# A residual-stream norm: statistics token-major, scale and shift in fused multiplies, and the first two weight chunks interleaved by k tile

## The reference, cut to what matters

```python
def rms_norm(x, eps=EPS):
    xf = x.astype(jnp.float32)
    return (xf * lax.rsqrt(jnp.mean(xf * xf, axis=-1, keepdims=True) + eps)).astype(x.dtype)

def adaln(x, mod, k):
    return rms_norm(x) * (1 + mod[:, :, k + 1]) + mod[:, :, k]

def swiglu(h, w_in, w_out):
    g, u = jnp.split(h @ w_in, 2, axis=-1)
    return (jax.nn.silu(g) * u) @ w_out
# in each layer: ffn, mixer, ffn
h = h + 0.5 * mod[:, :, 2] * swiglu(adaln(h, mod, 0), ffn_in[i, 0], ffn_out[i, 0])
```

## Time and profile before

| | |
|---|---|
| median of 3 runs | 2378.21 us (2377.03 to 2379.68) |
| the profiled execution | 2379.09 us, span 2377.3 us, mean granted TensorE clock 0.942 |
| TensorE busy | 2146.5 us, 90% of the span (10458 matmuls) |
| VectorE, ScalarE, GpSimd busy | 1534.8, 718.7, 312.4 us |
| chain that ended last | TensorE 73%, VectorE 13%, issue 5%, DMA 3%, ScalarE 3%, GpSimd 2% |
| the three lines of `mm3` in that chain | 22% each |

### The profile page before, as it was taken

One profiled execution on the slowest core, in us unless ns is written; L12 is line 12 of the kernel. 1 busy time (PEld: TensorE's weight loads), 2 busy tenths in 40 slices (PEclk: granted clock), 3 DMA queues, 4 the chain that ended last, 5 costly groups with the idle time before them and its releaser, 6 DMA issues.

```text
span 2377.3 us, 26622 instructions
## 1 busy us (share of the span) xinstructions
PE 2146.5 (90%) x10458; PEld 1773.2 (75%) x10458; DVE 1534.8 (65%) x2030; ACT 718.7 (30%) x886; POOL 312.4 (13%) x243
## 2 busy tenths in 40 slices
PE   3979999997998887999998999999799787887998
PEld 2657888885877775888886788888587784477997
DVE  4767666678886557676577766677644548944544
ACT  1223322223220022322222323222354433433443
POOL 1221000112003232000012000011200004541001
PEclk7669999999999998999999999999899898989999
DMA  4453443553450023444354444354223312334554
GB/s 151 142 177 124 142 144 111 156 156 106 142 189 7 1 89 105 143 132 151 109 168 131 133 151 142 95 168 150 83 88 98 124 58 63 98 106 142 178 159 126
DMA packets 297501, 293.28 MB, mean 123 GB/s; under 512 B 8903, under 2 KB 260720, under 8 KB 296304
## 3 DMA queue, kind: packets, MB, share of 16 engines
q1 hardware_dynamic: 292928, 278.62, 37.3%
q10 hardware_dynamic: 4464, 13.15, 1.5%
HBM read 285.38 MB, written 6.36 MB: 123 GB/s over the span
## 4 chain that ended last, share of the span: by engine, by line
PE 73%; DVE 13%; issue 5%; DMA 3%; ACT 3%; POOL 2%; ACTq 1%; POOLq 0%; DVEq 0%; SPq 0%
PE bank L1509 22%; PE bank L1511 22%; PE bank L1510 22%; DVE pp L971 3%; DVE wl L893 2%; PE bank L1729 2%; ACT wh L578 2%; DMA raw<-in_ffn_out 2%; DVE pp L968 1%; DMA raw<-in_ada_w 1%; PE bank L1647 1%; DVE early_av L428 1%; POOL acc L1430 1%; PE bank L1797 1%; POOL mm L1492 1%
## 5 line engine op out<-in xcount | busy, mean ns | idle before, releaser
L1509 PE MATMUL bank<-xh,wh 128*128 128x512 f32 (+1 forms) x2120 | 785.7, 371 | 76.9 <-POOL xl L1413 37.8
L1510 PE MATMUL bank<-xl,wh 128*128 128x512 f32 (+1 forms) x2120 | 776.7, 366 | 0.0
L1511 PE MATMUL bank<-xh,wl 128*128 128x512 f32 (+1 forms) x2120 | 776.2, 366 | 0.0
L893 DVE TENSOR_TENSOR wl<-raw,wh 128x2048 fp32r<-128x2048 f32 (+1 forms) x204 | 421.4, 2067 | 303.1 <-ACT wh L578 302.8
L578 ACT ACTIVATE wh<-raw 128x2048 fp32r<-128x2048 f32 (+1 forms) x204 | 353.7, 1735 | 595.9 <-PE bank L1511 507.7
L1509 PEld LDWEIGHTS bank<-xh,wh 128*128 128x128 f32 x2120 | 408.0, 192 | 157.7 <-issue 39.5
L1511 PEld LDWEIGHTS bank<-xh,wl 128*128 128x128 f32 x2120 | 407.2, 192 | 63.9
L1510 PEld LDWEIGHTS bank<-xl,wh 128*128 128x128 f32 x2120 | 408.3, 193 | 61.4
L1509 PE MATMUL bank<-gh,wh 128*128 128x512 f32 (+1 forms) x704 | 255.6, 363 | 2.9 <-DVE wl L893 1.5
L1510 PE MATMUL bank<-gl,wh 128*128 128x512 f32 (+1 forms) x704 | 255.2, 362 | 0.0
L1511 PE MATMUL bank<-gh,wl 128*128 128x512 f32 (+1 forms) x704 | 255.2, 362 | 0.0
(11 more groups left out here) (219 smaller groups left out, 2213.4 us busy)
## 6 DMA issues: line engine op xcount, KB each, us to landing
raw<-in_ffn_in SPq DMA_DIRECT2D x88, 1024.0 KB, 5.1
raw<-in_ffn_out SPq DMA_DIRECT2D x64, 704.0 KB, 4.7
ada_rawf<-in_ada_w SPq DMA_DIRECT2D x60, 512.0 KB, 4.5
ada_rawo<-in_ada_w SPq DMA_DIRECT2D x48, 512.0 KB, 4.3
raw<-in_mb_in_w SPq DMA_DIRECT2D x24, 1024.0 KB, 5.4
raw<-in_ada_w SPq DMA_DIRECT2D x12, 1024.0 KB, 5.0
raw<-in_hy_in_w SPq DMA_DIRECT2D x12, 1024.0 KB, 5.1
afb<-decays SPq DMA_DIRECT2D x32, 256.0 KB, 3.2
```

What stands on the lines that cost most here:

```text
L893: dve.tensor_tensor(wl[n_slot][:, 0:cols], raw[r_slot][:, 0:cols], wh[n_slot][:, 0:cols].bitcast(F32), ALU.subtract).then_inc(w_lo, 1)
L1509: pe.matmul(dst, h, x_hi, start=start, stop=False)
L1510: pe.matmul(dst, h, x_lo, start=False, stop=False)
L1511: return pe.matmul(dst, l_, x_hi, start=False, stop=stop)
```

## The change

- The eighth square is no longer added by GpSimd. TensorE sums `acc` and the eighth square in two groups of matmuls, with the data as the stationary side and one column of ones as the moving one, so that a token's sum lies in its partition: 128x4 instead of 4x128. Square root and reciprocal work on 128x4; four transposes of a broadcast column fill `bank[7]`.
- VectorE makes `xt` = `hT` x scale x `bank[7]` in one fused operation for each half of the tokens (`scaled`), ScalarE makes `xh` as Identity with the shift as its bias, and VectorE, no longer GpSimd, makes `xl` = (`xt` + shift) - `xh` in place, fused as well (`low`). `xt` lies where `xl` lies, so there is no wait for slots of `pp`. VectorE's order is scaled(0), scaled(1), low(0), scaled(2), low(1) and so on.
- For "00", "hy", "01", "10", "mb" and "11" TensorE works off chunks 0 and 1 together (`first_pair`): for each k tile four output tiles, twelve matmuls. `SHARED = DT`: over all eight k tiles.
- Chunk 1 is split before the norm: its high half by ScalarE ahead of the square root, its low half by GpSimd (`second_lo`). In pair 0 of an FFN VectorE's first step is the low half of chunk 2. In `HYIN` and `XB` the halves of chunk 1 leave the first step of pair 0.
- The final norm's two operations a tile become one fused one.
- The loops of `XB`, of `wide` and of GpSimd's adds are unrolled.

```diff
@@ scalar
             def norm(key, n=NT):
...
-                act.activation(rs[0:j, 0:P], bank[7][0:j, 0:P], ACT.Sqrt, bias=eps[0:j, 0:1],
+                act.activation(rs[:, 0:j], bank[7][:, 0:j], ACT.Sqrt, bias=eps[:, 0:1],
                                scale=1.0 / D).then_inc(rms_done, 1)
-            def norm_hi(key, n=NT):
+            def norm_hi(key, layer, k0, n=NT):
                 pl = norms[key]
                 for k in range(DT):
-                    hi_tile(pl.q + k, pl.q + k + 1, xh[:, k, 0:n], pp[(pl.q + k) % 2][:, 0:n])
+                    act.wait_ge(p_ready, pl.q + k + 1)
+                    for w in range(n // L):
+                        ins = act.activation(xh[:, k, w * L:w * L + L], xt[:, k, w * L:w * L + L], ACT.Identity,
+                                             bias=mods[layer][:, DT * k0 + k, w:w + 1])
+                    ins.then_inc(p_hi, 1)
-            def ffn(key, ada, after, n=NT):
+            def ffn(key, layer, k0, ada, after, n=NT):
+                pi, po = ffn_in[key], ffn_out[key]
+                next_hi(pi, 0, 0, 2)
                 norm(key, n)
-                norm_hi(key, n)
+                norm_hi(key, layer, k0, n)
...
-                pi, po = ffn_in[key], ffn_out[key]
-                next_hi(pi, 0, 0, 2)
@@ vector
             def norm(key, layer, k0, n=NT):
...
+                def scaled(k):
+                    for w in range(n // L):
+                        tok = slice(w * L, w * L + L)
+                        ins = dve.scalar_tensor_tensor(xt[:, k, tok], hT[:, k, tok], m[:, DT * (k0 + 1) + k, w:w + 1],
+                                                       bank[7][:, tok], ALU.mult, ALU.mult)
+                    ins.then_inc(p_ready, 1)
+                def low(k):
+                    dve.wait_ge(p_hi, pl.q + k + 1)
+                    for w in range(n // L):
+                        tok = slice(w * L, w * L + L)
+                        ins = dve.scalar_tensor_tensor(xl[:, k, tok], xt[:, k, tok], m[:, DT * k0 + k, w:w + 1],
+                                                       xh[:, k, tok].bitcast(F32), ALU.add, ALU.subtract)
+                    ins.then_inc(p_lo, 1)
+                scaled(0)
                 for k in range(DT):
-                    q = pl.q + k
...
+                    if k + 1 < DT:
+                        scaled(k + 1)
+                    low(k)
...
                 def pair(i, last):
-                    next_lo(pi, i, 0, 2) if not last else split_lo((pi.w + 1) % 2, pi.w + FT, CW, (pi.raw + 1) % 2)
+                    if last:
+                        split_lo((pi.w + 1) % 2, pi.w + FT, CW, (pi.raw + 1) % 2)
+                    else:
+                        next_lo(pi, i, 0 if i else 1, 2)
...
-                    else:
+                    elif i:
                         next_lo(pi, i, 1, 2)
@@ gpsimd
-            def norm_lo(key, n=NT):
...
+            def second_lo(pl):
+                pool.wait_ge(raw_in[pl.raw % 2], (pl.raw // 2 + 2) * 16)
+                pool.wait_ge(w_hi, pl.w + 2)
+                n = (pl.w + 1) % 2
+                pool.tensor_tensor(wl[n][:], raw[(pl.raw + 1) % 2][:], wh[n][:].bitcast(F32), ALU.subtract).then_inc(w_lo, 1)
@@ tensor
             def norm(key, n=NT):
                 pl = norms[key]
-                pe.wait_ge(acc_done, pl.h)
...
+                cols = n // P
+                pe.wait_ge(acc_done, pl.h - 1)
+                for j in range(cols):
+                    pe.matmul(bank[7][:, j:j + 1], acc[:, j * P:j * P + P], ones[:, 0:1], start=j == 0, stop=False)
+                pe.wait_ge(sq_done, pl.h)
+                for j in range(cols):
+                    ins = pe.matmul(bank[7][:, j:j + 1], tt[1][:, j * P:j * P + P], ones[:, 0:1], start=False, stop=j == cols - 1)
...
                 pe.wait_ge(rms_inv, pl.norm + 1)
-                for j in range(rows_):
-                    ins = pe.matmul(bank[7][:, j * P:j * P + P], ident[0:rows_, j:j + 1].to_broadcast([rows_, P]),
-                                    rs[0:rows_, 0:P], start=True, stop=True)
+                for j in range(cols):
+                    ins = pe.transpose(bank[7][:, j * P:j * P + P], rs[:, j:j + 1].to_broadcast([P, P]), ident)
                 ins.then_inc(rms_bc, 1)
+            def first_pair(pl, q, n=NT):
+                def tiles(u, k):
+                    for s in range(2):
+                        ins = mm3(bank[2 * u + s][:, 0:n], (pl.w + u) % 2, k * 256 + s * P, xh[:, k, 0:n], xl[:, k, 0:n],
+                                  k == 0, k == DT - 1)
+                    if k == DT - 1:
+                        ins.then_inc(w_used, 1)
+                for k in range(DT):
+                    pe.wait_ge(p_lo, q + k + 1)
+                    for u in range(2 if k < SHARED else 1):
+                        if k == 0:
+                            pe.wait_ge(w_lo, pl.w + u + 1)
+                        tiles(u, k)
+                for k in range(SHARED, DT):
+                    tiles(1, k)
```

More of the change, by code:

```diff
@@ L784, in xb_pair @@
                     split = lambda: (split_hi(DTP.w, 8 * P, DTP.raw % 2, DTP.raw // 2 + 1, DTP.w - 1)
-                                     if last and u == 1 else next_hi(XB, i, u, 2))
+                                     if last and u == 1 else next_hi(XB, i, u, 2) if i or u else None)
                     conv_chunk(XB, i, u, 12, split, lambda m: xb[:, :, m, :], NT)
-            steps(act, 6, xb_pair)
+            for i in range(6):
+                xb_pair(i, i == 5)
             split_hi(CP.w, CW, CP.raw % 2, CP.raw // 2 + 1, CP.w - 1)
@@ L955, in invert_rms @@
                 j = n // P
[L956 removed]
+                dve.reciprocal(rs[:, 0:j], rs[:, 0:j]).then_inc(rms_inv, 1)
                 dve.wait_ge(rms_bc, pl.norm + 1)
@@ L1231, in xb_pair @@
                         taps(XB, i, u, s, NT)
-            steps(dve, 6, xb_pair, own, 4)
+            for i in range(6):
+                xb_pair(i, i == 5)
             open_lo(CP)
@@ L1438, in add_squares @@
                     for i in range(DT // 2):
-                        for um in range(2):
+                        for um in range(2 if i < DT // 2 - 1 else 1):
                             pool.wait_ge(sq_done, 2 * i + um + 1)
@@ L1444, in add_squares @@
                 else:
-                    with pool.Fori(0, DT // 2) as i:
-                        for um in range(2):
+                    for i in range(DT // 2):
+                        for um in range(2 if i < DT // 2 - 1 else 1):
                             add_square(pl, i, um, n)
             def ffn(key, zeroed, n=NT):
-                norm_lo(key, n)
                 pi = ffn_in[key]
+                second_lo(pi)
                 pool.wait_ge(p_lo, pi.q + FT)
@@ L1570, in pair @@
                 def pair(i):
-                    for u in range(2):
+                    if i == 0:
+                        pe.wait_ge(gate_ready, pi.gate)
+                        first_pair(pi, x0, n)
+                    for u in range(2 if i else 0):
                         pe.wait_ge(w_lo, i * 2 + (pi.w + u + 1))
@@ L1676, in hy_pair @@
             def hy_pair(i, last):
-                for u in range(2):
+                if i == 0:
+                    pe.wait_ge(z_free, HYIN.zf)
+                    first_pair(HYIN, norms["hy"].q)
+                for u in range(2 if i else 0):
                     pe.wait_ge(w_lo, i * 2 + (HYIN.w + u + 1))
@@ L1753, in pair @@
                 def pair(i, last):
-                    for u in range(2):
+                    if pl is XB and i == 0:
+                        pe.wait_ge(free, base)
+                        first_pair(pl, x0)
+                    for u in range(0 if pl is XB and i == 0 else 2):
                         pe.wait_ge(w_lo, i * 2 + (pl.w + u + 1))
@@ L1757, in pair @@
                         two_tiles((pl.w + u) % 2, 2 * u, x0, n=n)
-                steps(pe, chunks // 2, pair)
+                for i in range(chunks // 2):
+                    pair(i, i == chunks // 2 - 1)
             wide(XB, 12, conv_free, XB.conv, NT)
```

48 lines of the change are left out of this document (19 added, 29 removed).

## The result

The changed kernel takes 2386.3 us (median) against 2378.6 for the one before: a ratio of 1.0031, 95% interval 1.0019 to 1.0043. The forecast was 2365, with a range of 2356 to 2377. It is slower by 0.3%, where I had forecast 0.6% faster. The profiled execution has a span of 2387.4 us at a granted clock of 0.933, before 2377.3 at 0.942.

A forecast was written before the change was run, and what follows sets the result against it. TensorE was taken as the bound, so only its idle or lower-clock time could be won. Gains of 0.7, 6.3, 1.4, 2.4, 2.1, -2.8 and 2.8 us in seven norms made some 13 us: 2365 us, range 2356 to 2377.

The forecast's parts named there:

- the start of GpSimd's pass: Chunk 1's low half in "10": starts at 1290.5 as ScalarE's high half ends, finishes at 1295.1 as VectorE's first is due.
- The pass's length: GpSimd's low half of chunk 1, 128x2048: about 4.55 us, with an upper bound of 8.5.
- Rival 2: Long GpSimd pass holds VectorE's first low half; gain gone from 6.8 us. 6 to 7.5 us: 12 in 100; longer: 8.
- The lock: VectorE's operations with two SBUF inputs stand during GpSimd's pass; without this "01" and "11" would be some 3.6 us better.
- The chain to T: Norm steps from the square root's table load to the first matmul: 4.25 us after that load, 2.27 earlier in "10".
- T: Start of a norm's first matmul; in "10" forecast at 1296.05, 2.27 us earlier than before.
- The refill: New wait before chunk 2, as slots free late: 4.05 us in FFNs, 4.2 in "11", 5.8 in "hy", 7.7 in "mb".
- rival 3: At chunk 2 the wait is longer, since the SiLU's table load (1.28 us) sits behind it: 2370 us, 14 in 100.
- the lower clock in the first pair: Chunks 0 and 1 together lose 1.8 us, half of some 3.6 us at TensorE's lower clock.
- The last norm: At the end, eight scalings of 0.353 us leave VectorE and the chain before is shorter: 2.8 us gained.
- Rival 4: TensorE still waits for k tiles, as VectorE's four operations take over 2.76 us: near 2375 us, 3 in 100.
- Rival 1: The clock is not lost at the waits for chunk 2; five charges of 1.8 us go: 2356 us, 8 in 100.

The follow-up runs named there:

- quarters: The changed kernel with GpSimd's late pass over chunk 1 split into four instructions of 512 columns: 2382.9 us, ratio 1.0010 to the kernel before.
- the early pass: The changed kernel with GpSimd's pass waiting for VectorE's low half of chunk 0, not chunk 2's landing: 2373.5 us, ratio 0.9967 to the kernel before.
- the rewrite alone: The changed kernel with the interleave undone, chunk 1's halves back behind the norm's and no GpSimd pass: 2325.5 us, ratio 0.9772 to the kernel before.

## Why the prediction was wrong, point by point

- **The step that failed** is the start of GpSimd's pass: in "10" I had it run "from 1290.5 to 1295.1", "just clear" of the first low half. I let it start with chunk 1's high half. It waits for chunk 2's load, issued only when VectorE has split chunk 0, and 7.4 us under way: in "10" of the changed kernel it starts 4.8 us behind that high half, and VectorE's first pair of low halves takes 5.17 us for 0.88. Moving that start alone changed the median from 2386.3 to 2373.5 (15 us by the ratios). Of my miss of 21 us this is the larger part.
- **The pass's length** was right: 4.55 forecast, 4.51 measured. Rival 2 had the right place and the right sign, slower because VectorE's first low half stands, but the wrong variable: its turning point was a pass of 6.8 us. A pass of 4.5 us that starts 4.8 us late does the same.
- **The lock** was right and its price is what was lost. By the Trainium skill (SBUF — State Buffer, "Who interferes with whom") a VectorE operation with two SBUF inputs and a GpSimd operation that reads SBUF exclude each other for a whole instruction. The traces agree in number: 4764 ns beside a pass of 4.5 us, 1581 beside quarters of 1.3 to 1.5, 488 without. The same section spares an operation with at most one SBUF input, and L977 (its other input in PSUM) takes 1.66 us for four pieces at 1288.10, beside a pass that ran to 1289.75.
- **The chain to T** was right in its parts: square root 0.26 (0.25), reciprocal 0.18 (0.2), transposes 0.65 at the higher clock and 1.12 at the lower (1.0), high half 0.91 (0.8), low half 0.87 (0.9). With the pass early, T is 8.3 us behind the last residual; before it was 10.4, so 2.1 earlier, where I wrote 2.27. In "01" and "11" T is 10.2 and 7.3 behind the last residual there, where my numbers gave 10.3 and 7.5: with the start of the pass put right, all six T come out as forecast.
- **The refill** was right: 3.94 for 4.05 in "01" and "10", 4.15 for 4.2 in "11", 5.81 for 5.8, 7.31 for 7.7. Only in "00" it took 5.27. There the SiLU's table load sits behind the wait, which is rival 3, in one stage of four:

```profile
199.52 1.28 ACT L629 ACT_TABLE_LOAD   x1 [13.25 <-issue]
```

- **Chunk 4** was left out, and the lower clock in the first pair put too low. With the early pass chunk 2 of "10" starts at 1318.74 and the third pair of SiLUs at 1355.37, 36.6 us later; before, chunk 2 starts at 1317.16 + 11.0 and that pair at 1361.92, 33.8 us later:

```profile
1344.14 0.50 PE L1533 MATMUL bank<-xh,wh 128*128 128x512 f32 x1 [0.82 <-DVE wl L902]
...
1355.37 1.09 ACT L629 ACTIVATE tt<-bank 128x512 f32<-128x512 f32 x2 [9.42 <-PE bank L1535]
```

```profile
1361.92 1.09 ACT L623 ACTIVATE tt<-bank 128x512 f32<-128x512 f32 x2 [8.77 <-PE bank L1511]
```

  Of the 2.9 us, 0.8 is a wait at chunk 4, where I had found enough time at chunk 3 and looked no further, and 1.8 the clock in chunk 2, just as charged; 0.3 is left over. From T to T the stage was to gain 2.4 us by my terms and gained 1.2 with the early pass (385.95 against 384.73). Some 5 us still lie between 2365 and what the early pass measured by its ratio. They stand between T and chunk 2: 29.8, 30.6, 28.9, 27.8, 31.7 and 18.6 us in the six norms of that run, where I had 27.95, 29.7, 27.95, 27.95, 31.6 and 17.3, together 5.0 more. Of these 1.2 is the table load in "00"; most of the rest is a longer stretch at the lower clock behind T, 12 or 13 matmuls of 0.63 us or more in "00", "hy" and "01" where "10" has 8.
- **The last norm** brought about the 2.8 us forecast: its stretch from the last residual to the end is 2.7 us shorter. **Rival 4** did not occur: no wait between k tiles inside the first pair once both chunks are there. **Rival 1** fell: of six waits at chunk 2 five are followed by a matmul at the lower clock. In "11" the first two after 4.15 us take 0.39 and 0.28 (256 columns), and the lower clock (0.41) follows from there on. The length of the wait alone doesn't say when the clock falls: after the same 3.94 us "01" of the early pass starts with 0.50, and the lower clock (0.63) comes from the sixth matmul on:

```profile
935.29 0.50 PE L1533 MATMUL bank<-xh,wh 128*128 128x512 f32 x1 [3.94 <-DVE wl L902]
```

  The prediction named two rows for the cost of a wait. The one after 3.32 us shows 0.50, which is quick; in that trace too the lower clock (0.63) comes later, from the seventh matmul on.
- **What the sum hid.** It priced the change as a whole against the kernel before and found 13 us. It never priced the rewrite alone. Its own terms held the answer: 4 us of refill and 1.8 of clock in each norm, against an interleave that wins only what VectorE's new pace leaves. By the ratios, the rewrite gives -54 us, the full interleave with chunk 1's high half ahead of the square root +46, and the late start of the pass +15.

## What to carry to other kernels

Read each wait's number, not only its name: which transfer does that count stand for, who issues it, and when does it land in the trace at hand? Work that is split between two engines is safe from their mutual hold only if its place in time is known as well as its length. Price each half of a change by itself: here one half wins 2.3%, and the other gives back 1.9% by itself and another 0.6% by its late start, since an interleave that frees both buffers at one moment buys a refill, and sharing only the first tiles does not.

## What was new of the hardware

- The mutual hold of VectorE and GpSimd can be read off one line's statistics. A low half of 0.47 us took up to 4.76 us beside one GpSimd instruction of 4.5 us, and GpSimd's four quarters took 5.76 us with VectorE's two-input operations between them, where four of the shortest quarters in that run, 1.26 each, make 5.0.
- GpSimd gets in between two VectorE operations that stand back to back: the pair began at 1302.24, the pass ran from 1302.63 to 1307.12, and the second piece, 4.76 us long, ended at 1307.41, so by the trace it had begun at 1302.65 and stood for the whole of the pass.
- Four transposes of 128x128 take 0.65 us at the higher clock (granted 1.00 over 1299.70 to 1300.40, norm "10" of the changed kernel) and 1.12 at the lower (granted 0.50 over 558.84 to 560.00, its norm "hy").
- GpSimd starts 0.14 us after the semaphore that releases it, even after 14 us of idling (1285.24 behind a high half that ended at 1285.10).
